# Two layers on one core: order of the work in three inner norms, and in the opening of the first feed-forward part

## The reference, cut to what matters

```
x = x + rms_norm(mixed @ w_out, post_mix_norm)          # joint 1 begins
h = rms_norm(x, pre_ffn_norm)                           # joint 1 ends
u = causal_dwconv(h @ ffn_w_up, ffn_conv_w, ffn_conv_b) # 3 taps along the tokens
gate, val = split(u, 2)
f = (gelu(gate) * val) @ ffn_w_down
x = x + rms_norm(f, post_ffn_norm)                      # joint 2: then a norm and w_in_2
...                                                     # second layer: attention, joint 3,
u = square(relu(h @ w_up)); x = x + rmsnorm(u @ w_down, ln_mlp_post)
```

## Time and profile before

| | |
|---|---|
| median of 3 timed runs | 932.22 us (930.96 to 933.86) |
| profiled execution, its own time | 934.1 us |
| its span, first to last instruction | 932.3 us |
| PE busy | 875.4 us, 94% of the span |
| DVE, ACT, POOL busy | 596.2, 463.9, 78.4 us |
| mean granted clock of TensorE | 0.98 |

### The profile page before, as it was taken

The page is one execution under the profiler, slowest core; times in us unless marked ns, Lnnn a source line. Parts: engine busy times, 40 slices in busy tenths (PEclk is TensorE's granted clock), DMA queues, the critical chain, the costliest instruction groups (busy, mean ns, idle before and its releaser), DMA issues.

```text
span 932.3 us, 15563 instructions
## 1 busy us (share of the span) xinstructions
PE 875.4 (94%) x6246; PEld 809.9 (87%) x6246; DVE 596.2 (64%) x765; ACT 463.9 (50%) x648; POOL 78.4 (8%) x78
## 2 busy tenths in 40 slices
PE   3999897999999999889999999889998899999997
PEld 3999797999988899789999999779985799999995
DVE  4348756535777578669676776766645576556654
ACT  5356763236856534457455555464444454433332
POOL 0025661100000032000000000000000000000000
PEclk9999898999999999999999999999998999999999
DMA  8442333142433435626555456253321435555541
GB/s 321 170 181 91 136 136 136 54 149 104 143 136 130 153 141 181 226 95 233 181 181 192 173 185 217 91 181 136 103 79 68 180 133 207 181 185 190 196 150 46
DMA packets 21736, 143.83 MB, mean 154 GB/s; under 512 B 3008, under 2 KB 3012, under 8 KB 5168
## 3 DMA queue, kind: packets, MB, share of 16 engines
q1 hardware_dynamic: 19872, 138.30, 41.5%
q0 software_dynamic: 1808, 4.73, 1.5%
HBM read 141.96 MB, written 1.84 MB: 154 GB/s over the span
## 4 chain that ended last, share of the span: by engine, by line
PE 81%; DVE 9%; ACT 4%; issue 3%; DMA 1%; POOL 1%; SPq 0%; ACTq 0%; DVEq 0%; POOLq 0%
PE pj L467 16%; PE pj L469 13%; PE pj L470 13%; PE pa L862 6%; PE pa L863 6%; PE pa L864 6%; DVE area L1555 3%; PE pj L471 2%; DVE w_lo L1542 2%; PE pj L472 2%; PE pa L506 2%; PE pj L562 1%; PE pj L563 1%; PE pj L564 1%; DVE area L1558 1%
## 5 line engine op out<-in xcount | busy, mean ns | idle before, releaser
L467 PE MATMUL pj<-a_hi,w_hi 128*128 128x256 f32 x1184 | 340.3, 287 | 12.0 <-DVE w_lo L1542 9.1
L1542 DVE TENSOR_TENSOR w_lo<-w_raw,w_hi 128x2048 fp32r<-128x2048 f32 x128 | 300.1, 2347 | 76.9 <-ACT w_hi L1101 76.9
L469 PE MATMUL pj<-a_lo,w_hi 128*128 128x256 f32 x1184 | 337.0, 285 | 0.0
L470 PE MATMUL pj<-a_hi,w_lo 128*128 128x256 f32 x1184 | 336.8, 284 | 0.0
L1101 ACT ACTIVATE w_hi<-w_raw 128x2048 fp32r<-128x2048 f32 x128 | 243.8, 1906 | 74.1 <-PE pa L864 43.3
L467 PEld LDWEIGHTS pj<-a_hi,w_hi 128*128 128x128 f32 x1184 | 229.2, 194 | 17.0 <-issue 16.0
L469 PEld LDWEIGHTS pj<-a_lo,w_hi 128*128 128x128 f32 x1184 | 229.3, 194 | 0.9
L470 PEld LDWEIGHTS pj<-a_hi,w_lo 128*128 128x128 f32 x1184 | 229.1, 193 | 0.0
L862 PE MATMUL pa<-w_hi,a_hi 128*128 128x512 f32 x280 | 110.2, 394 | 1.8 <-issue 1.8
L863 PE MATMUL pa<-w_lo,a_hi 128*128 128x512 f32 x280 | 110.0, 393 | 0.0
L864 PE MATMUL pa<-w_hi,a_lo 128*128 128x512 f32 x280 | 109.7, 392 | 0.0
(11 more groups left out here) (247 smaller groups left out, 1069.2 us busy)
## 6 DMA issues: line engine op xcount, KB each, us to landing
w_raw<-stream SPq DMA_DIRECT2D x128, 1024.0 KB, 4.8
area<-gains POOLq DMA_DIRECT2D x4, 512.0 KB, 3.9
cst<-consts SPq DMA_DIRECT2D x1, 1093.0 KB, 14.0
x_tok<-x_in SPq DMA_DIRECT2D x2, 512.0 KB, 4.6
area<-cmpw POOLq DMA_DIRECT2D x1, 1024.0 KB, 5.5
out<-x_tok SPq DMA_DIRECT2D x4, 256.0 KB, 2.0
t_wide<-t_rows POOLq DMA_DIRECT2D x1, 768.0 KB, 13.3
prm<-params SPq DMA_DIRECT2D x1, 562.5 KB, 10.3
```

The source lines that it names most:

```text
L467: pe.matmul(out_, a[0], a[1], start=first, stop=False)
L469: pe.matmul(out_, wh, al, start=False, stop=False)
L470: return pe.matmul(out_, wl, ah, start=False, stop=last)
L1542: dve.tensor_tensor(w_lo[:, slot, :], w_raw[:, slot, :], w_hi[:, slot, :].bitcast(F32), ALU.subtract)\
```

## The change

Norms: DVE adds the left halves of both token halves first, makes `a_hi` and `a_lo` of blocks 0 and 1, and only then takes the right half of the first tokens, `a_lo` of block 2, and the right half of the second tokens. Quarter 1 is turned into bank 2, quarter 2 into bank 1 (`turned`). In the pair, blocks 0 and 1 start on a new semaphore `x_hi`, raised after `a_hi[k]`; the eight matmuls that need only `a_hi` come first, the four with `a_lo` behind them. `keep_warm` moves ahead of the other transposes of the left half; the transposes of quarters 2 and 3 move from behind block 1 to behind block 2. In the diff the first opening (with `up1_tap2`) is ACT's, the last (with `up1_out`) DVE's. Opening: ACT runs one Gelu on one element ahead of all, then the fourth unit's `w_hi`, then the first taps; DVE reads out chunks 0 and 1 together, and makes `w_lo` of the fourth and fifth unit ahead of where it did.

```diff
+        def turned(j, k):
+            q = k // 2
+            return pa[:, (0, 2, 1, 3)[q] if j else q, (k % 2) * T:(k % 2 + 1) * T]
...
             def first_pair(j, u, b):
                 turn_x(j, 0, 0, 1)
+                keep_warm(2, WARM)
+                turn_x(j, 0, 1, 2)
                 turn_x(j, 1, 0, 2)
-                keep_warm(2, WARM)
-                turn_x(j, 0, 1, 3)
-                turn_x(j, 1, 1, 4)
+                turn_x(j, 1, 1, 3)
...
                 for k in range(KC):
-                    if k == 2:
-                        for q in (2, 3):
-                            turn_x(j, q, 0, 5)
-                            turn_x(j, q, 1, 5)
-                    gate(k)
+                    if k == 3:
+                        turn_x(j, 2, 0, 4)
+                        turn_x(j, 2, 1, 5)
+                        turn_x(j, 3, 0, 5)
+                        turn_x(j, 3, 1, 5)
+                    if k < 2:
+                        pe.wait_ge(S("x_hi"), 2 * j + k + 1)
+                    else:
+                        gate(k)
...
                         for nb in range(2):
+                            first_hi(pj[b[i][0]][:, nb * T:(nb + 1) * T], (u + i) % SLOTS, k * 256 + nb * P, k, nb == 0)
+                    if k < 2:
+                        gate(k)
+                    for i in range(2):
+                        for nb in range(2):
+                            mm = first_lo(pj[b[i][0]][:, nb * T:(nb + 1) * T], (u + i) % SLOTS, k * 256 + nb * P, k)
...
+            def first_hi(o_, slot, c, k, fresh):
+
+                pe.matmul(o_, w_hi[:, slot, c:c + P], a_hi[:, k, :], start=(k == 0 and fresh), stop=False,
+                          skip_group_check=True)
+                pe.matmul(o_, w_lo[:, slot, c:c + P], a_hi[:, k, :], start=False, stop=False, skip_group_check=True)
+
+            def first_lo(o_, slot, c, k):
+
+                return pe.matmul(o_, w_hi[:, slot, c:c + P], a_lo[:, k, :], start=False, stop=(k == KC - 1),
                                  skip_group_check=True)
...
             u0 = U_FFN1
-            for c in range(4):
+            act.activation(warm, eps_t, ACT.Gelu_apprx_tanh)
+            ahead(u0 + 1)
+            up1_tap2(0, 0, FFN1_BANK0[0], 0)
+            up1_tap2(1, 1, FFN1_BANK0[1], 1)
+            ahead(u0 + 2)
+            up1_gelu(0, 0)
+            up1_hi(0, 8, 0)
+            up1_gelu(1, 1)
+            for c in (2, 3):
                 up1_tap2(c, c % 3, FFN1_BANK0[c % 3] + c // 3, c % 2)
-                if c:
-                    up1_hi(c - 1, 8 + c - 1, (c - 1) % 2)
+                up1_hi(c - 1, 8 + c - 1, (c - 1) % 2)
                 ahead(u0 + 1 + c)
                 up1_gelu(c, c % 2)
...
+            def y_norm(j, gname):
+                dve.wait_ge(S("gbc_loaded"), 16 * (j + 1))
+                y_bias(j, 0)
+                y_recip(j, 0)
+                x_add(0, 0, 512, "x_ready")
+                y_bias(j, 1)
+                y_recip(j, 1)
+                x_add(1, 0, 256, "x_ready")
+                x_add(1, 256, 512, "x_ready")
...
+                y_gain(j, 0, 1)
+                x_add(0, 512, 1024, "x_ready")
+                operand_lo(j + 1, gname, 2)
+                y_gain(j, 1, 1)
+                x_add(1, 512, 1024, "x_ready")
+                for k in range(3, KC):
+                    operand_lo(j + 1, gname, k)
...
             u0 = U_FFN1
-            for c in range(4):
+            up1_out(0, u0 + 1, 0)
+            up1_out(1, u0 + 2, 1)
+            ahead(u0 + 1)
+            up1_taps(0, 0, FFN1_BANK0[0], 0)
+            ahead(u0 + 2)
+            up1_product(0, 0)
+            up1_taps(1, 1, FFN1_BANK0[1], 1)
+            up1_lo(0, 8, 0)
+            for c in (2, 3):
                 up1_out(c % 3, u0 + c + 1, c % 2)
-                if c:
-                    up1_product(c - 1, (c - 1) % 2)
-                    ahead(u0 + c)
+                up1_product(c - 1, (c - 1) % 2)
+                if c == 2:
+                    ahead(u0 + 3)
                 up1_taps(c, c % 3, FFN1_BANK0[c % 3] + c // 3, c % 2)
```

More of the change, by code:

```diff
@@ L528, in turn_x @@
                 for k in (2 * q, 2 * q + 1):
-                    o = (k % 2) * T + tb * P
-                    mm = transpose(pa[:, q, o:o + P], x_tok[:, tb, k * P:(k + 1) * P])
+                    mm = transpose(turned(j + 1, k)[:, tb * P:(tb + 1) * P], x_tok[:, tb, k * P:(k + 1) * P])
                 if tb == 1:
@@ L1130, in operand @@
                         await_psum(act, "ST"[k // 4], "x")
-                    act.activation(a_hi[:, k, :], pa[:, k // 2, (k % 2) * T:(k % 2 + 1) * T], ACT.Copy,
-                                   scale=g[:, k:k + 1]).then_inc(S("opnd_hi"), 1)
+                    act.activation(a_hi[:, k, :], turned(j, k), ACT.Copy, scale=g[:, k:k + 1]).then_inc(S("opnd_hi"), 1)
             def x_squares(j, junk_):
@@ L1576, in operand_lo @@
                 dve.wait_ge(S("opnd_hi"), (k | 1) + 1 + (6 * j if j else 0))
-                stt(a_lo[:, k, :], pa[:, k // 2, (k % 2) * T:(k % 2 + 1) * T], g[:, k:k + 1],
-                    a_hi[:, k, :].bitcast(F32), ALU.mult, ALU.subtract).then_inc(S("opnd_lo"), 1)
+                stt(a_lo[:, k, :], turned(j, k), g[:, k:k + 1], a_hi[:, k, :].bitcast(F32), ALU.mult, ALU.subtract)\
+                    .then_inc(S("opnd_lo"), 1)
             def x_spread(j, before_rbc=None):
@@ L1601, in x_add, with y_bias, y_recip @@
                     .then_inc(S(done), 1)
-            def y_norm(j, gname=None):
+            def y_bias(j, tb):
+                dve.wait_ge(S("y_sq"), 4 * j + 2 * tb + 1)
+                dve.tensor_scalar(ybias[:, tb:tb + 1], ysum[:, 2 * tb:2 * tb + 1], 1.0 / D, EPS, ALU.mult, ALU.add)\
+                   .then_inc(S("y_bias"), 1)
+                y_gain(j, tb, 0)
+            def y_recip(j, tb):
+                dve.wait_ge(S("rms_root"), 2 * j + tb + 1)
+                V_.did(dve.reciprocal(yr[:, tb:tb + 1], yrt[:, tb:tb + 1]))
+                V_.sync()
@@ L1606, in y_norm, with y_final @@
+            def y_final(j):
                 dve.wait_ge(S("gbc_loaded"), 16 * (j + 1))
                 for tb in range(2):
[L1608 to L1632, removed]
@@ L1633, in y_norm @@
-                    y_gain(j, tb, 1)
[L1634 to L1637, removed]
+                    y_bias(j, tb)
+                    y_recip(j, tb)
+                    x_add(tb, 0, 512, "x_final")
+                    y_gain(j, tb, 1)
+                    x_add(tb, 512, 1024, "x_final")
+            def y_norm(j, gname):
[7 more added lines that the diff above has]
+                x_add(1, 256, 512, "x_ready")
+                g = prm_(gname)
+                dve.wait_ge(S("x_turned"), 4 * j + 1)
+                for k in range(2):
+                    dve.tensor_scalar(a_hi[:, k, :], turned(j + 1, k), g[:, k:k + 1], None, ALU.mult)\
+                       .then_inc(S("x_hi"), 1)
+                    dve.wait_ge(S("x_hi"), 2 * j + k + 1)
+                    stt(a_lo[:, k, :], turned(j + 1, k), g[:, k:k + 1], a_hi[:, k, :].bitcast(F32), ALU.mult,
+                        ALU.subtract).then_inc(S("opnd_lo"), 1)
+                y_gain(j, 0, 1)
[5 more added lines that the diff above has]
+                    operand_lo(j + 1, gname, k)
@@ L2180, in _ @@
             ffn2_step(UP2 - 1, UP2 // 3, 0)
-            y_norm(3)
+            y_final(3)
 def pack(v):
```

6 lines of the change are left out of this document (1 added, 5 removed).

## The result

The changed kernel takes 924.67 us (median of 4 runs, 923.88 to 925.52) against 932.69 for the kernel before; the ratio is 0.9903, interval 0.9879 to 0.9928. Its profiled execution took 925.52 us, 8.6 less than that of before.

What follows compares the result with a forecast made beforehand. TensorE, holding 81% of the chain, was taken to bound the kernel. From a median of 932.2, 2.3 (first norm and opening), 1.15 (second norm) and 0.85 (third norm) came off: 927.9 us, range 925.3 to 931.0.

Steps and rivals of the forecast that it cites:

- the limit that took 0.6 of the 1.45 us away: First norm: the pair ends 1.45 us earlier, but the third unit waits for its w_lo, so only 0.85 is gained.
- the two gaps of VectorE: Opening: DVE waits 3.0 us for the sixth unit's w_hi, then 0.9 us for the taps of chunk 3.
- the new wait at the first `down`: End of the opening: PE waits 1.7 us ahead of the first down for the seventh unit's w_lo.
- the 2.3 us for norm and opening: First norm and opening together gain 2.3 us up to the first down, not 0.85 + 2.94.
- Third norm: Same picture as the first norm, the third unit limited by its w_lo: 0.85 us gained.
- the bounds of the opening: Gain to the first down: 4.0 us without DVE's gaps, 0.3 with gaps half as long again, 1.5 with a slower table load.
- The sum: Whole kernel: 928.35 us from the profiled execution, 927.9 from the median, 926.5 if the median had the low clock.
- So I take it out of both: Second norm: 1.42 us of low clock removed from the profiled excess over the median and from the gain.
- 1.15: Second norm: the gain in us where the clock does not fall either way, against 2.6 with the low clock removed.
- (C): Norms: the pair starts earlier but waits for a_lo at blocks 1 to 3; only 1.0 gained, 931.2 us; chance 0.06.
- (E): Pairs: PE idles in small pieces and the clock falls to 1.2 GHz, making the kernel slower; chance 0.04.
- (D): Opening: more gain than forecast, under 926 us, because DVE's gaps close; chance 0.08.

Runs made afterwards that it cites:

- e1: The kernel before, unchanged, profiled and timed a second time: 933.69 us, ratio 1.0016.
- e3: The kernel before with only the new feed-forward opening on ScalarE and VectorE, norms as before: 933.53 us, ratio 1.0004.
- e4: The kernel before with only keep_warm moved ahead of the second pair of transposes in the norms: 931.62 us, ratio 0.9981.
- e13: The kernel before with five idle matmuls directly behind the second norm's pair, ahead of the second layer's attention: 933.25 us, ratio 0.9996.
- e14: The kernel before with nine idle matmuls directly behind the second norm's pair, ahead of the second layer's attention: 934.23 us, ratio 1.0024.
- e12: The kernel before with more idle matmuls between each norm's first two pairs of transposes, keep_warm where it was: 929.89 us, ratio 0.9968.
- e8: The changed kernel with idle matmuls where PE waits in the second layer's attention: 923.91 us, ratio 0.9889 to the kernel before.
- e16: The changed kernel with the additions of e7 and e8 and without keep_warm in the three norms: 921.45 us, ratio 0.9874 to the kernel before.
- e9: The changed kernel without keep_warm in the three norms: 924.06 us, ratio 0.9915 to the kernel before.
- e5: The changed kernel, unchanged, profiled and timed a second time: 926.44 us, ratio 0.9913 to the kernel before.
- e7: The changed kernel with the sixth unit's w_hi on ACT ahead of the second Gelu and third taps: 925.61 us, ratio 0.9899 to the kernel before.

## Why the prediction was wrong

**The mechanics were right.** Each link of the first norm came within 0.2 us (a unit's 5.76 us was worked out from 417.53, where the row has 417.46: 0.02 us, without effect), and so did the limit that took 0.6 of the 1.45 us away (the third unit's `w_lo`), the two gaps of VectorE, the new wait at the first `down` and the 2.3 us for norm and opening (2.42). Third norm 0.98 against 0.85. None of the bounds of the opening was needed.

**What failed is the step "The sum".** It has two errors, both about low clock.

1. "So I take it out of both": I took the 1.42 us of low clock in the second norm to be absent from the median. It is in all six profiles with the old order there and no added matmuls in the norm (before, e1, e3, e4, e13, e14), and e12, which adds nothing but idle matmuls in the norms, is 3 us faster in the median (part of that may lie in the attention part: its profile gains 1.41 in the second norm and 2.35 there). Whether every timed run has the stretch no run shows. In the profile the term is 2.80, and not 1.15: 1.65 us too little.

2. The attention part stood in the sum at nothing, as an untouched part. It is where 2.19 us of the profiled gain lie. Low clock there costs 4.9 us before and 2.7 after (against the 127.5 of e8), and how much depends on where its first stretch begins, counted from the part's start. In the changed kernel, where all that is ahead ends 5.3 us earlier, that point stood at 18.1 us in both profiles, and in the kernel before at 19.8 and 19.3. That the earlier end is what moved it is argued, not shown. I had the row that the clock can fall in the second norm, and did not ask for the other places with the same cost in the same trace; the waits of 3.1 and 1.5 us in the attention part stood in it.

The working from the profile, 928.35 against a profiled 925.52, would have missed by 2.8: 2.19 of it the attention part. Taking out the low clock made it 3.2 against the median.

**Rivals.** (C), "doesn't do what it says", fell: `a_lo` of block 2 held PE up by 0.16 us, less than the 0.3 reckoned. (E), low clock in a pair: it did come, with the old order in e1, e3, e4 and e14, and with the new one in e16, which lacks `keep_warm`; in no profile with the new order and the call. (D), more than forecast, was right in sign and wrong in cause: VectorE's gaps are there as reckoned. And what I took for certain about `keep_warm`, that its new place holds the clock, was not the reason: moved alone it did not in e4's profile, and the changed order holds the clock in one profile without it (e9) and not in another (e16). What fits all of them is that PE is idle for less time in the norm (1.61 us against 3.08); no run isolates it. With the new order and the call, none of nine profiles has low clock in the second norm.

**Open.** Whether a given stretch of the program has low clock varies from run to run: single times of the kernel before went from 930.46 to 938.73, and e1 and e14 had two stretches more than the first profile. How the 2 us of the attention part divide over all timed runs isn't settled; the profiles are one run each. That they are in the median too is argued from the sum: 2.4 + 2.8 + 1.0 is 6.2, and the medians differ by 8.0 in the result and by 7.8 in e5. On record is also the mean granted clock of every timed run. Of the changed kernel's ten, both profiled ones and five others have 0.986 and three have 0.980 or 0.982; of 35 of the kernel before, taken together with e1 to e4, five have 0.985 and take 930.5 to 930.7 us, 3.4 less than the profiled one. No profile shows where the low clock stands in those. So the cause of the 2.19 us is known as far as this: it is low clock in an untouched part. What places it is open.

## What to carry to other kernels

Read the granted clock over the whole trace before a sum is made, list every low stretch with the waits ahead of it, and put each into the sum as a term that can be there or not after an edit anywhere ahead of it. Where TensorE had to wait for 1 to 3 us, idle matmuls in the wait itself cost nothing here and held the clock in two profiles of three (13 of them won 2.7 us; in e16 a stretch came at a place without a wait); moving the norm's idle matmuls out of the wait won nothing in the second norm of e4's profile. Compare a part in more than one profile before its time is called the kernel's. And where a late split is brought forward, follow the engine's own order to the next consumer but two: the wait came back three units later, and one more split moved (e7) took it away.

## What the runs showed of the hardware

In the parts compared here TensorE's clock stood at 1.2 GHz for 3.4 us at a time, or twice that, also where PE had been busy right up to it in the profile's sense: at 682.5 in the kernel before, PE's busy time was full on both sides. Just ahead of it, from 680.13, stood sixteen matmuls (as the profile counts them) of one column each, in 1.84 us. In e4's pair the matmuls of 256 columns took 0.41 us at 1.2 GHz, one every 0.21, against 0.28 and one every 0.12 at 2.4. The changed kernel's two profiles have their stretch in the attention part at 620.8 and 620.9 us, and six profiles of five kernels have it 19.3 to 19.8 us into that part, so it is not scattered evenly over the runs.
